# A hybrid attention layer on one core: the first transfers in smaller pieces, and the first row of the first contraction ordered by part

## The chip, the cores and the metric

The kernel runs on one core of a Trainium2 chip. The metric is the device time of one execution in microseconds. Five engines work beside one another, each through its own list of instructions, and wait for one another by semaphores: TensorE (PE, products; PEld is its weight load), VectorE (DVE), ScalarE (ACT), GpSimd (POOL), and SyncE (SP), which only issues transfers. The order inside each list is written out by hand.

## What is computed

One layer of an encoder, on a batch of 512 tokens and one of 256, with the same weights; all values are 32-bit floats.

```
h = x @ w_in                       # 1024 -> 3328 columns, for eight groups of columns
qa, ka, va, ga, qb, kb, vb, gb = split(h)
out_a = dilated_attention(rope(qa), rope(ka), va) * silu(ga)      # 8 heads of 64
out_b = gqa_attention(axial_rope(rms_norm(qb)), axial_rope(rms_norm(kb)), vb) * silu(gb)
f = concat(out_a, out_b) @ w_out
y = layer_norm(alpha * x + f)
```

## The kernel before

**Three products for one.** Every operand of a product is split into a high part, its value rounded to the format that TensorE reads, and a low part, the difference to the value itself. A product of two operands is made of three on TensorE: low by high, high by low, high by high (`three`, line 519). ScalarE makes the high parts by a copy (`weights_high` line 706, `x_high` line 736), VectorE and GpSimd the low parts by a subtraction (`x_low` line 901; `weights_low` line 906 on VectorE, line 1151 on GpSimd).

**Tiles.** x comes transposed, as 8 rows of the contraction (k = 0 to 7), each 128 partitions by 768 tokens, 384 KB, loaded into `mix_t[:, k, :]`; its parts are `t_hi` and `t_lo`. The weights come as 34 units of 128 partitions by 1024 columns, 512 KB. Units are loaded into `raw` (two slots; units 2 and 3 go into `prob`), and their parts lie in `w_hi` and `w_lo`, three slots each.

**The first stage.** `natural(chunk, k)` (line 528) multiplies row k of x, six tiles of 128 tokens, with the weights of a chunk: chunk 0 is the keys and values of mixer B (256 columns, units 0 and 1, four rows k in each), chunks 1 and 2 have 512 columns and two rows to a unit. Each of the six tiles has a PSUM bank, and adds up over k. For each k the order is tile by tile, with the three products of a tile behind one another. Before a row TensorE waits for the low part of that row of x (line 534) and for the low part of the weights (lines 536 and 538). Then follow further projections, run between the steps of the attention, the attention itself, the output product and the layer norm.

**The order at the start.** ScalarE issues the first half of unit 0 on its own queue (line 826; 512 columns, rows k = 0 and 1). SyncE issues, one after another: x of rows 0 and 1, the second half of unit 0, x of rows 2 and 3, unit 1, x of rows 4 to 7, unit 2, tables, unit 3 and the rest. Unit 4 takes the slot of unit 0, and so waits until both low halves of unit 0 are made (line 475). ScalarE then makes the high parts in this order: first half of unit 0, x 0, x 1, second half of unit 0, x 2, x 3, unit 1, x 4 to x 7, units 2 and 3. VectorE makes the low part of the first half of unit 0 and then of x 0 to x 7 (line 1058), GpSimd that of the second half (line 1225) and of units 1 to 3. `hi_count`, `on_dve` and `lo_taken` (lines 282 to 292) work out the counts that each of the semaphores must have reached.

In this document row k (row 0, row 1, ...) is a step of the contraction; [rows 3] is a group of rows of the trace.

Of the kernel before, what the change touches and what calls it, by code (L numbers as in the profile page):

```python
# [7 lines left out]
F32 = mybir.dt.float32  # L8
F32R = mybir.dt.float32r
ALU = mybir.AluOpType  # L10
# [4 lines left out]
P = 128  # L15
# [25 lines left out]
UW = 1024  # L41
# [114 lines left out]
def build(nc, xt, x_prompt, x_sample, weights, q_norm, k_norm, ln_g, ln_b, consts, consts_b, y_prompt, y_sample):  # L156
    ctx = ExitStack()
    with ctx:
# [3 lines left out]
        def sem(name):  # L162
            return ctx.enter_context(nc.semaphore(name))
# [47 lines left out]

        x_loaded = [sem(f"x_loaded{k}") for k in range(KT)]
        ident_loaded, consts_loaded, tables_loaded = sem("ident_loaded"), sem("consts_loaded"), sem("tables_loaded")
        raw_first = sem("raw_first")
        raw_loaded = [sem(f"raw_loaded{i}") for i in range(EARLY)]
        xt_hi, xt_lo = sem("xt_hi"), sem("xt_lo")
        w_hi_done, w_lo_pool, w_lo_dve = sem("w_hi_done"), sem("w_lo_pool"), sem("w_lo_dve")
# [61 lines left out]
            return tuple(a[at // 512][:, at % 512:at % 512 + n] for a in (hi, lo))  # L279


        def hi_count(g, half=1):
            return half + 1 if g == 0 else g + 2

        def on_dve(g, half=0):
            return (g == 0 and half == 0) or NAT_UNITS > g >= KV_UNITS + Q_UNITS or (g >= FIRST_OUT + 3 and g % 2 == 0)

        def lo_taken(g, half=1):
            order = [(0, 0), (0, 1)] + [(n, 1) for n in range(1, UNITS_W)]
            upto = order[:order.index((g, half)) + 1]  # L290
            mine = on_dve(g, half)
            return (w_lo_dve if mine else w_lo_pool), sum(1 for n, s in upto if on_dve(n, s) == mine)


# [172 lines left out]
        def _(sp):  # L467
# [3 lines left out]
            def load_unit(g):  # L471
                if g >= EARLY:
                    sp.wait_ge(*lo_taken(raw_before(g)))
                if g == EARLY:
                    sp.wait_ge(*lo_taken(0, 0))
                sp.dma_start(raw_slot(g), weights[g]).then_inc(raw_arrival(g)[0], 16)

            load_x(0)
            load_x(1)
            sp.dma_start(raw_slot(0)[:, 512:UW], weights[0][:, 512:UW]).then_inc(raw_loaded[0], 16)  # L480
            load_x(2)
            load_x(3)
            load_unit(1)
# [34 lines left out]
        def _(pe):  # L518
# [6 lines left out]
            def x_cols(k, cols):  # L525
                return t_hi[:, k, cols], t_lo[:, k, cols]

            def natural(chunk, k):
                width = 2 * KV_WIDTH if chunk == 0 else CW
                rows = UW // width  # L530
                first, n_units = natural_units(chunk)
                g, row = first + k // rows, k % rows
                if chunk == 0:
                    pe.wait_ge(xt_lo, k + 1)
                if g == 0:
                    pe.wait_ge(*lo_taken(0, row * width // 512))
# [123 lines left out]
                if m == KT - 1:  # L660
                    ins.then_inc(acc_ready, 1)

            for k in range(KT):
                natural(0, k)
            for k in range(KT):
                natural(1, k)
# [36 lines left out]

        @block.scalar
        def _(act):
            def weights_high(g, half=None):
                if half == 0:
                    act.wait_ge(raw_first, 16)
                else:
                    act.wait_ge(*raw_arrival(g))  # L710
# [7 lines left out]
                if half is not None:  # L718
                    nc.scalar.activation(hi[half], raw_slot(g)[:, 512 * half:512 * (half + 1)], ACT.Copy) \
                        .then_inc(w_hi_done, 1)  # L720
                else:
                    nc.scalar.activation(both(hi, g), raw_slot(g), ACT.Copy).then_inc(w_hi_done, 1)  # L722

            def both(hi, g):
                n = g - FIRST_OUT - RING
                if n < 0:
                    return w_hi[:, g % RING, :]
                if n == 0:
                    return k_st[:].rearrange("p s a t -> p (s a t)")[:, 0:UW]
                if n == 1:  # L730
                    return q_st[:].rearrange("p s t -> p (s t)")[:, 0:UW]
                if n in (2, 3):
                    return p_hi[:, n - 2].rearrange("p a c -> p (a c)")
                return v_st[:].rearrange("p s t d -> p (s t d)")[:, 0:UW]

            def x_high(k):
                act.wait_ge(x_loaded[k], 16)
# [85 lines left out]
                if kind(b) == "g":  # L823
                    gate_tanh(b, part)

            act.dma_start(raw_slot(0)[:, 0:512], weights[0][:, 0:512]).then_inc(raw_first, 16)
            weights_high(0, 0)
            x_high(0)
            x_high(1)
            weights_high(0, 1)  # L830
            x_high(2)
            x_high(3)
            weights_high(1)
# [59 lines left out]
        def _(dve):  # L893
# [5 lines left out]
                dve.wait_ge(dve_step, links[0])  # L899

            def x_low(k):
                dve.wait_ge(xt_hi, k + 1)
# [3 lines left out]
            def weights_low(g, half=None):  # L906
                dve.wait_ge(w_hi_done, hi_count(g, 1 if half is None else half))
                hi, lo = unit_places(g)
                for n in range(2) if half is None else (half,):
# [145 lines left out]
                    .then_inc(mix_lo_dve, 1)  # L1055

            nc.vector.memset(zero[:], 0.0)
            weights_low(0, 0)
            for k in range(KT):
                x_low(k)  # L1060
            gain_tables()
            for chunk in range(2):
# [80 lines left out]
        def _(pool):  # L1143
# [4 lines left out]
                ins.then_inc(pool_step, 1)  # L1148
                pool.wait_ge(pool_step, links[0])

            def weights_low(g, half=None):
                pool.wait_ge(w_hi_done, hi_count(g, 1 if half is None else half))
                hi, lo = unit_places(g)
                if half is not None:
                    nc.gpsimd.tensor_tensor(lo[half], raw_slot(g)[:, 512 * half:512 * (half + 1)],
                                            hi[half].bitcast(F32), ALU.subtract).then_inc(w_lo_pool, 1)
                    return
# [64 lines left out]
                nc.gpsimd.tensor_tensor(t_lo[:, e, :], mix_t[:, e, :], t_hi[:, e, :].bitcast(F32), ALU.subtract) \  # L1222
                    .then_inc(mix_lo_pool, 1)

            weights_low(0, 1)
            for g in range(1, 4):
                weights_low(g)
            for t in range(TILES):
# [68 lines left out]
```

## Time and profile before

| | us |
|---|---|
| median of 3 runs | 455.47 (453.39 to 456.83) |
| the profiled execution, its own time | 455.87 |
| its span, first instruction to last | 453.9 |
| TensorE busy with products | 408.9 (90%) |
| VectorE, ScalarE, GpSimd busy | 307.2, 233.8, 227.5 |

All times in the rows are from the profiled execution and count from the beginning of its span. A row of the timeline gives start, length, engine, line of the kernel, operation, and what is written from what; in square brackets how long the engine sat idle before it, and what ended that. A product's printed length contains its way through the array, so that products overlap: their rate is read from their starts.

### The profile page before, as it was taken

The numbers are of one execution on the slowest core, as the hardware profiler recorded it, in microseconds if no ns is written. First come the engines' busy times: TensorE is split into PE (matmuls) and PEld (weight loads), VectorE is DVE, ScalarE is ACT, GpSimd is POOL, SyncE is SP. The second block draws the span as 40 slices with busy tenths as digits, with TensorE's granted clock in tenths as the row PEclk, the third lists the DMA queues.
The fourth block names the chain that finished last, engine by engine and source line by source line (L and its number), as shares of the span: only waits on it lengthen the run. The fifth ranks groups of instructions, "written<-read, shape, count | busy, mean of one in ns | idle before, by whom it ended". The sixth has DMA issues, their size and how long they took to land.

```text
span 453.9 us, 6757 instructions
## 1 busy us (share of the span) xinstructions
PE 408.9 (90%) x2350; PEld 354.2 (78%) x2350; DVE 307.2 (68%) x711; ACT 233.8 (52%) x466; POOL 227.5 (50%) x232
## 2 busy tenths in 40 slices
PE   3999999979988999999999999999898499999970
PEld 3988888768977888888879898888787378888860
DVE  4653237946778886676698998875865634554987
ACT  5441044045656766767677575576574746221331
POOL 1655051474655365455548678845753856221221
PEclk9999999989999999999999999999998979999995
DMA  8821201112011011011011011401110134210113
GB/s 301 340 76 55 75 17 48 47 56 83 4 46 45 3 48 45 3 46 48 2 46 48 1 46 48 140 5 43 48 46 3 46 134 191 92 48 0 71 73 134
DMA packets 10112, 30.11 MB, mean 66 GB/s; under 512 B 1376, under 2 KB 1504, under 8 KB 10080
## 3 DMA queue, kind: packets, MB, share of 16 engines
q1 hardware_dynamic: 9936, 29.43, 18.5%
q8 instruction: 19, 0.31, 0.3%
q10 hardware_dynamic: 144, 0.26, 0.2%
q14 instruction: 13, 0.11, 0.1%
HBM read 26.54 MB, written 3.15 MB: 65 GB/s over the span
## 4 chain that ended last, share of the span: by engine, by line
PE 51%; DVE 26%; issue 8%; ACT 8%; POOL 5%; DMA 1%; DVEq 0%; ACTq 0%; POOLq 0%
PE bank L521 13%; PE bank L522 12%; PE bank L523 12%; PE bank L637 6%; PE bank L568 4%; DVE prob L996 3%; DVE p_lo L1010 3%; ACT prob L782 2%; DVE k_st L976 2%; POOL w_lo L1159 2%; DVE h L1129 2%; DVE q_st L976 2%; ACT w_hi L722 2%; DVE mix_t L1017 2%; PE bank L596 1%
## 5 line engine op out<-in xcount | busy, mean ns | idle before, releaser
L1209 POOL TENSOR_SCALAR prob<-prob,den 128x512 f32<-128x512 f32 (+1 forms) x96 | 68.1, 716 | 60.1 <-DVE den L1005 59.9
L521 PE MATMUL bank<-t_hi,w_lo 128*128 128x512 f32 (+1 forms) x256 | 87.5, 342 | 1.5 <-POOL w_lo L1159 1.5
L523 PE MATMUL bank<-t_hi,w_hi 128*128 128x512 f32 (+1 forms) x256 | 87.0, 340 | 0.0
L522 PE MATMUL bank<-t_lo,w_hi 128*128 128x512 f32 (+1 forms) x256 | 87.0, 340 | 0.0
L1159 POOL TENSOR_TENSOR w_lo<-raw,w_hi 128x512 fp32r<-128x512 f32 x44 | 60.9, 1407 | 49.3 <-ACT w_hi L722 49.3
L791 ACT ACTIVATE p_hi<-bank 128x512 fp32r<-128x512 f32 x80 | 47.8, 597 | 67.9 <-PE bank L568 67.0
L521 PE MATMUL bank<-w_hi,t_lo 128*128 128x512 f32 (+1 forms) x180 | 67.4, 374 | 13.9 <-DVE t_lo L903 7.9
L1010 DVE TENSOR_TENSOR p_lo<-bank,p_hi 128x512 fp32r<-128x512 f32 x80 | 55.1, 689 | 36.3 <-ACT p_hi L791 35.2
L782 ACT ACTIVATE prob<-prob,nmax 128x512 f32<-128x512 f32 (+1 forms) x96 | 62.1, 647 | 32.6 <-DVE nmax L996 32.0
L522 PE MATMUL bank<-w_lo,t_hi 128*128 128x512 f32 (+1 forms) x180 | 66.6, 370 | 0.0
L523 PE MATMUL bank<-w_hi,t_hi 128*128 128x512 f32 (+1 forms) x180 | 66.4, 369 | 0.0
L637 PE MATMUL bank<-p_hi,v_st 128*128 128x256 f32 x160 | 46.5, 308 | 13.1 <-DVE p_lo L1010 8.8
L521 PEld LDWEIGHTS bank<-t_hi,w_lo 128*128 128x128 f32 x256 | 48.7, 190 | 7.9 <-POOL w_lo L1159 1.7
L522 PEld LDWEIGHTS bank<-t_lo,w_hi 128*128 128x128 f32 x256 | 48.8, 191 | 6.2
L523 PEld LDWEIGHTS bank<-t_hi,w_hi 128*128 128x128 f32 x256 | 48.8, 190 | 5.7
L521 PEld LDWEIGHTS bank<-w_hi,t_lo 128*128 128x128 f32 x180 | 35.4, 197 | 19.7 <-DVE t_lo L903 7.9
L568 PE MATMUL bank<-cst,prob 128*128 128x128 f32 x320 | 48.0, 272 | 0.1
L722 ACT ACTIVATE w_hi<-raw 128x1024 fp32r<-128x1024 f32 x26 | 27.3, 1051 | 34.8 <-PE bank L523 19.5
L568 PEld LDWEIGHTS bank<-cst,prob 128*128 128x128 f32 x320 | 38.7, 140 | 7.4 <-POOL prob L1209 0.5
L637 PEld LDWEIGHTS bank<-p_hi,v_st 128*128 128x128 f32 x160 | 30.5, 191 | 16.9 <-issue 11.1
L523 PEld LDWEIGHTS bank<-w_hi,t_hi 128*128 128x128 f32 x180 | 35.4, 197 | 5.4
L522 PEld LDWEIGHTS bank<-w_lo,t_hi 128*128 128x128 f32 x180 | 35.5, 197 | 5.0
(137 smaller groups left out, 771.5 us busy)
## 6 DMA issues: line engine op xcount, KB each, us to landing
raw<-weights SPq DMA_DIRECT2D x31, 512.0 KB, 3.3
mix_t<-xt SPq DMA_DIRECT2D x8, 384.0 KB, 7.1
h<-x_prompt SPq DMA_DIRECT2D x4, 512.0 KB, 5.2
y_prompt<-h SPq DMA_DIRECT2D x8, 256.0 KB, 2.0
prob<-weights SPq DMA_DIRECT2D x2, 512.0 KB, 10.8
h<-x_sample SPq DMA_DIRECT2D x2, 512.0 KB, 8.7
y_sample<-h SPq DMA_DIRECT2D x4, 256.0 KB, 2.0
cst<-consts SPq DMA_DIRECT2D x1, 960.0 KB, 11.2
```

Of the source, the lines that this page charges most:

```text
L521: nc.tensor.matmul(out, a_lo, b_hi, start=first, stop=False)
L522: nc.tensor.matmul(out, a_hi, b_lo, start=False, stop=False)
L523: return nc.tensor.matmul(out, a_hi, b_hi, start=False, stop=last)
L568: ins = nc.tensor.transpose(dst[:, n * P:(n + 1) * P], src, ident)
L637: ins = nc.tensor.matmul(out, lhs, rhs, start=(n == 0 and rhs is hi), stop=(last and rhs is hi))
L722: nc.scalar.activation(both(hi, g), raw_slot(g), ACT.Copy).then_inc(w_hi_done, 1)
L782: ins = nc.scalar.activation(s, s, ACT.Exp, scale=-1.0, bias=nmax[:, j % 2, t:t + 1], accum_out=den[:, j % 2, t:t + 1])
L791: nc.scalar.activation(p_hi[:, slot, at, :], pt_ps[u % 2][:], ACT.Copy).then_inc(pt_hi_done, 1)
L976: nc.vector.tensor_tensor(by_tile(lo), src, by_tile(hi.bitcast(F32)), ALU.subtract).then_inc(staged_lo, 1)
L1010: nc.vector.tensor_tensor(p_lo[:, slot, at, :], pt_ps[u % 2][:], p_hi[:, slot, at, :].bitcast(F32), ALU.subtract).then_inc(pt_lo_done, 1)
L1159: ins = nc.gpsimd.tensor_tensor(lo[n], raw_slot(g)[:, 512 * n:512 * (n + 1)], hi[n].bitcast(F32), ALU.subtract)
L1209: ins = nc.gpsimd.tensor_scalar(s, s, den[:, j % 2, t:t + 1], 0.5, ALU.mult, ALU.mult)
```

## The change

Unit 0 is cut into three pieces (256, 256 and 512 columns) instead of two halves. The first belongs to row 0, the second to row 1, the third to rows 2 and 3. x of row 0 is loaded in two halves of 384 tokens (three tiles each) and rounded in two halves; its low part is still made at once. Row 0 has an order of its own, `first_row`: all six tiles high by high, then six high x by low weights, then six low x by high weights, each group behind its own wait. Rows 1 to 7 are done as before. VectorE makes the low parts of the first two pieces, with x 0 between them, GpSimd that of the third.

```diff
+        STARTS = (slice(0, 256), slice(256, 512), slice(512, UW))
...
-            load_x(0)
+            sp.dma_start(mix_t[:, 0, 0:3 * P], xt[:, 0, 0:3 * P]).then_inc(x_first, 16)
+            sp.dma_start(mix_t[:, 0, 3 * P:TOK], xt[:, 0, 3 * P:TOK]).then_inc(x_loaded[0], 16)
+            sp.dma_start(raw_slot(0)[:, STARTS[1]], weights[0][:, STARTS[1]]).then_inc(raw_second, 16)
             load_x(1)
-            sp.dma_start(raw_slot(0)[:, 512:UW], weights[0][:, 512:UW]).then_inc(raw_loaded[0], 16)
+            sp.dma_start(raw_slot(0)[:, STARTS[2]], weights[0][:, STARTS[2]]).then_inc(raw_loaded[0], 16)
             load_x(2)
...
                 if g == EARLY:
-                    sp.wait_ge(*lo_taken(0, 0))
+                    sp.wait_ge(*lo_taken(0, 1))
...
+            def first_row():
+                w_h, w_l = weight(0, 0, 2 * KV_WIDTH)
+                pe.wait_ge(w_hi_done, hi_count(0, 0))
+                for t in range(TILES):
+                    if t == 0:
+                        pe.wait_ge(x_first_hi, 1)
+                    elif t == 3:
+                        pe.wait_ge(xt_hi, 1)
+                    x_h, x_l = x_cols(0, slice(t * P, (t + 1) * P))
+                    nc.tensor.matmul(bank[t][:, 0:2 * KV_WIDTH], x_h, w_h, start=True, stop=False)
+                pe.wait_ge(*lo_taken(0, 0))
+                for t in range(TILES):
+                    x_h, x_l = x_cols(0, slice(t * P, (t + 1) * P))
+                    nc.tensor.matmul(bank[t][:, 0:2 * KV_WIDTH], x_h, w_l, start=False, stop=False)
+                pe.wait_ge(xt_lo, 1)
+                for t in range(TILES):
+                    x_h, x_l = x_cols(0, slice(t * P, (t + 1) * P))
+                    nc.tensor.matmul(bank[t][:, 0:2 * KV_WIDTH], x_l, w_h, start=False, stop=False)
...
-            for k in range(KT):
+            first_row()
+            for k in range(1, KT):
                 natural(0, k)
...
+            def first_high(step):
+                act.wait_ge((raw_first, raw_second, raw_loaded[0])[step], 16)
+                cols = STARTS[step]
+                nc.scalar.activation(w_hi[:, 0, cols], raw_slot(0)[:, cols], ACT.Copy).then_inc(w_hi_done, 1)
...
+            def first_x_high():
+                act.wait_ge(x_first, 16)
+                nc.scalar.activation(t_hi[:, 0, 0:3 * P], mix_t[:, 0, 0:3 * P], ACT.Copy).then_inc(x_first_hi, 1)
+                act.wait_ge(x_loaded[0], 16)
+                nc.scalar.activation(t_hi[:, 0, 3 * P:TOK], mix_t[:, 0, 3 * P:TOK], ACT.Copy).then_inc(xt_hi, 1)
...
-            act.dma_start(raw_slot(0)[:, 0:512], weights[0][:, 0:512]).then_inc(raw_first, 16)
-            weights_high(0, 0)
-            x_high(0)
+            act.dma_start(raw_slot(0)[:, STARTS[0]], weights[0][:, STARTS[0]]).then_inc(raw_first, 16)
+            first_high(0)
+            first_x_high()
+            first_high(1)
             x_high(1)
-            weights_high(0, 1)
+            first_high(2)
...
-            weights_low(0, 0)
-            for k in range(KT):
+            first_low(0)
+            x_low(0)
+            first_low(1)
+            for k in range(1, KT):
                 x_low(k)
...
-            weights_low(0, 1)
+            first_low(2)
```

How this moves the instructions is shown at two places; a row is a line of the kernel, an operation, what is written from what, its size, and in brackets the semaphores it waits for. On TensorE, at the beginning of its list, row 0 of chunk 0 stands before the change as triples (w_lo, t_hi and so on are the parts):

```order
L521 MATMUL bank<-w_hi,t_lo 128x256 [waits w_lo_dve,xt_lo]
L522 MATMUL bank<-w_lo,t_hi 128x256
L523 MATMUL bank<-w_hi,t_hi 128x256
L521 MATMUL bank<-w_hi,t_lo 128x256
L522 MATMUL bank<-w_lo,t_hi 128x256
```

and with the change, up to the first triple of row 1:

```order
L543 MATMUL bank<-w_hi,t_hi 128x256 [waits x_first_hi,w_hi_done]
L543 MATMUL bank<-w_hi,t_hi 128x256 x2
L543 MATMUL bank<-w_hi,t_hi 128x256 [waits xt_hi]
L543 MATMUL bank<-w_hi,t_hi 128x256 x2
L547 MATMUL bank<-w_lo,t_hi 128x256 [waits w_lo_dve]
L547 MATMUL bank<-w_lo,t_hi 128x256 x5
L551 MATMUL bank<-w_hi,t_lo 128x256 [waits xt_lo]
L551 MATMUL bank<-w_hi,t_lo 128x256 x5
L526 MATMUL bank<-w_hi,t_lo 128x256 [waits w_lo_dve,xt_lo]
```

The 18 products of the row are the same; the one wait that stood ahead of all of them is now four. On ScalarE, whose list begins with the first transfer of weights, this stands before:

```order
L826 DMA raw<-weights 128x512
L719 ACT_TABLE_LOAD
L719 ACTIVATE w_hi<-raw 128x512 [waits raw_first]
L738 ACTIVATE t_hi<-mix_t 128x768 [waits x_loaded0]
L738 ACTIVATE t_hi<-mix_t 128x768 [waits x_loaded1]
L719 ACTIVATE w_hi<-raw 128x512 [waits raw_loaded0]
L738 ACTIVATE t_hi<-mix_t 128x768 [waits x_loaded2]
```

and this with the change:

```order
L856 DMA raw<-weights 128x256
L735 ACT_TABLE_LOAD
L735 ACTIVATE w_hi<-raw 128x256 [waits raw_first]
L762 ACTIVATE t_hi<-mix_t 128x384 [waits x_first]
L764 ACTIVATE t_hi<-mix_t 128x384 [waits x_loaded0]
L735 ACTIVATE w_hi<-raw 128x256 [waits raw_second]
L768 ACTIVATE t_hi<-mix_t 128x768 [waits x_loaded1]
L735 ACTIVATE w_hi<-raw 128x512 [waits raw_loaded0]
L768 ACTIVATE t_hi<-mix_t 128x768 [waits x_loaded2]
```

Two roundings of whole tiles have become four of parts, and from x of row 2 on the list is the old one.

## Rows read from the trace of the kernel before

**Rows 1.** The chain that ended last, by engine, share of the span

```profile
PE 51%; DVE 26%; issue 8%; ACT 8%; POOL 5%; DMA 1%; DVEq 0%; ACTq 0%; POOLq 0%
```

**Rows 2.** The same chain in order of time, its beginning: start, length, what

```profile
0.73 4.74 DMA raw<-weights
...
5.50 0.63 ACT w_hi L719
6.12 0.74 ACT t_hi L738
...
6.89 0.97 DVE t_lo L903
...
7.90 0.58 PE bank L521
```

**Rows 3.** Waits of TensorE, 0 to 100 us: in total, times, longest

```profile
PE bank L521 <- DVE t_lo L903: 7.9, 1, 7.9
PE bank L521 <- POOL w_lo L1159: 1.5, 1, 1.5
```

**Rows 4.** Timeline of TensorE, its second product: start, length, line, operation

```profile
8.28 0.41 PE L522 MATMUL bank<-w_lo,t_hi 128*128 128x256 f32 x1
```

**Rows 5.** Busy time (instructions) by stretch, PE first; last: PEclk, transfer share, GB/s

```profile
0.00:3.50 3.50, 0.00 (x0) 0.00 (x0) 0.06 (x1) 1.28 (x1) 0.20 (x4) 1.00 0.46 78
3.50:4.50 1.00, 0.00 (x0) 0.00 (x0) 0.00 (x0) 0.00 (x0) 0.00 (x0) 1.00 1.04 369
...
7.90:12.55 4.65, 4.65 (x22) 4.65 (x22) 3.48 (x4) 3.84 (x6) 2.61 (x2) 1.00 1.03 413
12.55:20.00 7.45, 7.45 (x63) 7.45 (x63) 6.06 (x5) 3.49 (x4) 5.34 (x4) 1.00 0.80 309
```

**Rows 6.** Transfers by issue, up to 2 us: KB each, median us to landing

```profile
mix_t<-xt SPq DMA_DIRECT2D x1, 384.0 KB, 4.6
...
mix_t<-xt SPq DMA_DIRECT2D x2, 384.0 KB, 5.0
...
raw<-weights SPq DMA_DIRECT2D x1, 256.0 KB, 5.6
```

**Rows 7.** Timeline of SyncE's queue, its first issues

```profile
0.74 0.85 SPq L469 DMA_DIRECT2D mix_t<-xt  x2
1.64 0.42 SPq L480 DMA_DIRECT2D raw<-weights  x1
```

**Rows 8.** ScalarE's groups by shape, up to 100 us: busy, mean ns, idle before

```profile
L738 ACT ACTIVATE t_hi<-mix_t 128x768 fp32r<-128x768 f32 x8 | 6.6, 841 | 0.6
L744 ACT ACTIVATE hkv<-bank 128x256 f32<-128x256 f32 x6 | 2.2, 383 | 4.6 <-PE bank L523 4.6
...
L719 ACT ACTIVATE w_hi<-raw 128x512 fp32r<-128x512 f32 x2 | 1.2, 622 | 3.0 <-DMA raw<-weights 3.0
```

**Rows 9.** Timeline of ScalarE, VectorE and GpSimd, 6 to 15 us

```profile
6.03 1.56 ACT L738 ACTIVATE t_hi<-mix_t 128x768 fp32r<-128x768 f32 x2
...
8.19 1.67 POOL L1155 TENSOR_TENSOR w_lo<-raw,w_hi 128x512 fp32r<-128x512 f32 x1 [7.75 <-ACT w_hi L719]
...
9.10 2.45 DVE L903 TENSOR_TENSOR t_lo<-mix_t,t_hi 128x768 fp32r<-128x768 f32 x2 [0.38 <-ACT t_hi L738]
...
11.61 3.27 POOL L1159 TENSOR_TENSOR w_lo<-raw,w_hi 128x512 fp32r<-128x512 f32 x2 [1.75 <-ACT w_hi L722]
```

**Rows 10.** Timeline of VectorE, its two operations on 256 columns

```profile
18.82 1.30 DVE L918 TENSOR_TENSOR gate<-gate,norms 128x256 f32<-128x256 f32 x1 [1.39 <-DMA norms<-k_norm]
...
20.55 0.43 DVE L918 TENSOR_TENSOR gate<-gate,norms 128x256 f32<-128x256 f32 x1
```

**Rows 11.** Busy time by stretch, where the granted clock (last but two) first fell

```profile
97.80:101.40 3.60, 3.60 (x12) 2.77 (x11) 1.56 (x1) 0.00 (x0) 2.69 (x2) 0.53 0.47 146
```

**Rows 12.** The chain in order of time, 97 to 103 us

```profile
98.47 0.43 PE bank L521
...
102.19 0.24 PE bank L522
```

More of the change, by code:

```diff
@@ L213, in build @@
         ident_loaded, consts_loaded, tables_loaded = sem("ident_loaded"), sem("consts_loaded"), sem("tables_loaded")
-        raw_first = sem("raw_first")
+        raw_first, raw_second, x_first, x_first_hi = (sem("raw_first"), sem("raw_second"), sem("x_first"),
+                                                      sem("x_first_hi"))
         raw_loaded = [sem(f"raw_loaded{i}") for i in range(EARLY)]
@@ L279, in weight, with hi_count, on_dve, lo_taken @@
             return tuple(a[at // 512][:, at % 512:at % 512 + n] for a in (hi, lo))
[L282 to L291, printed above, removed]
+        STARTS = (slice(0, 256), slice(256, 512), slice(512, UW))
+        def hi_count(g, step=2):
+            return step + 1 if g == 0 else g + 3
+        def on_dve(g, step=2):
+            return (g == 0 and step < 2) or NAT_UNITS > g >= KV_UNITS + Q_UNITS or (g >= FIRST_OUT + 3 and g % 2 == 0)
+        def lo_taken(g, step=2):
+            order = [(0, 0), (0, 1), (0, 2)] + [(n, 2) for n in range(1, UNITS_W)]
+            upto = order[:order.index((g, step)) + 1]
+            mine = on_dve(g, step)
             return (w_lo_dve if mine else w_lo_pool), sum(1 for n, s in upto if on_dve(n, s) == mine)
@@ L535, in natural @@
                 if g == 0:
-                    pe.wait_ge(*lo_taken(0, row * width // 512))
+                    pe.wait_ge(*lo_taken(0, min(row, 2)))
                 elif row == 0:
@@ L705, in _, with weights_high @@
         def _(act):
[L706 to L710, printed above, removed]
+            def first_high(step):
+                act.wait_ge((raw_first, raw_second, raw_loaded[0])[step], 16)
+                cols = STARTS[step]
+                nc.scalar.activation(w_hi[:, 0, cols], raw_slot(0)[:, cols], ACT.Copy).then_inc(w_hi_done, 1)
+            def weights_high(g):
+                act.wait_ge(*raw_arrival(g))
                 if RING <= g < FIRST_OUT + RING:
@@ L717, in weights_high @@
                 hi = unit_places(g)[0]
[L718 to L722, printed above, removed]
+                nc.scalar.activation(both(hi, g), raw_slot(g), ACT.Copy).then_inc(w_hi_done, 1)
             def both(hi, g):
@@ L901, in x_low @@
             def x_low(k):
+                if k == 0:
+                    dve.wait_ge(x_first_hi, 1)
                 dve.wait_ge(xt_hi, k + 1)
@@ L904, in x_low, with first_low, weights_low @@
                     .then_inc(xt_lo, 1)
-            def weights_low(g, half=None):
-                dve.wait_ge(w_hi_done, hi_count(g, 1 if half is None else half))
+            def first_low(step):
+                dve.wait_ge(w_hi_done, hi_count(0, step))
+                cols = STARTS[step]
+                nc.vector.tensor_tensor(w_lo[:, 0, cols], raw_slot(0)[:, cols], w_hi[:, 0, cols].bitcast(F32),
+                                        ALU.subtract).then_inc(w_lo_dve, 1)
+            def weights_low(g):
+                dve.wait_ge(w_hi_done, hi_count(g))
                 hi, lo = unit_places(g)
-                for n in range(2) if half is None else (half,):
+                for n in range(2):
                     ins = nc.vector.tensor_tensor(lo[n], raw_slot(g)[:, 512 * n:512 * (n + 1)], hi[n].bitcast(F32),
@@ L1149, in after, with first_low, weights_low @@
                 pool.wait_ge(pool_step, links[0])
-            def weights_low(g, half=None):
-                pool.wait_ge(w_hi_done, hi_count(g, 1 if half is None else half))
+            def first_low(step):
+                pool.wait_ge(w_hi_done, hi_count(0, step))
+                cols = STARTS[step]
+                nc.gpsimd.tensor_tensor(w_lo[:, 0, cols], raw_slot(0)[:, cols], w_hi[:, 0, cols].bitcast(F32),
+                                        ALU.subtract).then_inc(w_lo_pool, 1)
+            def weights_low(g):
+                pool.wait_ge(w_hi_done, hi_count(g))
                 hi, lo = unit_places(g)
[L1154 to L1157, printed above, removed]
                 for n in range(2):
```

## The prediction

> **What bounds the kernel now.** I read the chain of work that ended last first. It is half TensorE and a quarter VectorE, and transfers hold only 1% of it [rows 1]. In order of time it begins with one transfer, the first half of the first weight unit: 4.74 us from its issue at 0.73 [rows 2]. Behind it stand three steps in a row, each on whole tiles: ScalarE rounds 512 weight columns (5.50), then 768 columns of x (6.12), VectorE subtracts to get the low part of x (6.89), and the first product starts at 7.90. From then on the chain is products. The list of TensorE's waits says the same: of all its idle time up to 100 us, 7.9 us stand before the first product, and the next entry has 1.5 us [rows 3]. So whatever starts the first product earlier moves the whole program, if two things hold: the operands of the later rows must not become the new wait, and TensorE must work at the same rate.
>
> The rate has two levels in the timeline. Between 7.90 and 12.55 stand 22 products of 256 columns; behind a first spacing of 0.38 (7.90 to 8.28 [rows 4]) that is 4.27 us for 20 spacings, 0.213 us each, or 256 columns at 1.2 GHz. From 12.55 to 20.00 stand 63 in 7.45 us, 0.12 us each: the level of 2.4 GHz [rows 5]. The lower level lasted 4.65 us, counted from the first product. (The table by stretches prints a granted clock of 1.00 for both; the spacing tells them apart.)
>
> **The first transfers.** Before, 256 KB of weights and 384 KB of x must land: 5.47, and 0.74 + 4.6 = 5.34 us [rows 2, 6]. After, 128 KB and 192 KB are enough for the first product. The table by stretches shows the transfer engines 46% busy up to 3.5 us, moving 3.5 x 78 = 273 KB, and full from then on, at 369 KB a microsecond [rows 5]. So 320 KB had been moved at 3.5 + 47 / 369 = 3.63, and 640 KB at 4.50, 0.87 us later. Pieces of the later transfers were among those bytes, before, and will be after; and shorter rows carry more overhead each. I take 0.72 us: landing at 4.75. No row shows loads of rows this short. The bounds: nothing gained (the slow beginning, not the bytes, sets 5.47; a later landing is excluded, since the same engines move fewer bytes ahead of it), or 1.2 us, when the slow beginning shrinks too. The value lies near the byte count because from 3.5 us on the engines are full.
>
> SyncE issues two transfers more ahead of x of row 1; two take 0.85 us on its queue [rows 7]. So everything behind them is issued that much later. That is hidden by the queue itself: x of row 1, issued about 1.17, took 5.4 us (the median over it and the first, 4.6, is 5.0) [rows 6], and the engines are full from 3.5 us, so work is queued there and issues are not lacking. If that cover were gone, x of row 1 would come at 7.4 instead of 6.6; rounding and subtracting take 1.8 us (0.84 [rows 8] and 0.97 [rows 2]), and TensorE wants it at 9.66, so it still fits.
>
> **From landing to the first product.** Before, 7.90 - 5.47 = 2.43 us. After, the first product needs only two roundings, of 256 and of 384 columns. 256 columns take ScalarE 0.38 us, 512 take 0.62, 768 take 0.84 [rows 8]; so 0.40 for the first (bounds 0.38 and 0.62) and 0.50 for the second, between 0.38 and 0.62. With 0.03 us at the front, an overlap of 0.1 that the two roundings at 5.50 and 6.03 show [rows 9], and 0.04 to the product: 0.03 + 0.40 - 0.10 + 0.50 + 0.04 = 0.87, or 0.9. That saves 1.53 us; together with the transfers 2.25. The first product starts at 5.65.
>
> **Does the first row then run without waits?** The new order is six products high by high, six with the low weights, six with the low x, at 0.213 us (first spacing 0.38): the groups start at 5.65, 7.3 and 8.6, and row 0 ends at 9.66. Product 4 (6.46) wants the second half of x: it lands 192 / 369 = 0.5 us after the first, at about 5.3, and is rounded from 5.6 to 6.1. The low weights: VectorE, 256 columns, 0.43 us [rows 10], from 5.2 to 5.65, against 7.3. The low x: 0.95 us from 6.14, done 7.1, against 8.6. None waits, by 0.3 to 1.6 us. A 256-column subtraction has also taken 1.30 us (beside GpSimd) [rows 10]; then the low x is done at 8.0, still in time. No product is added: 18 before, 18 after.
>
> **And the later rows?** VectorE does the second weight quarter after the low x (7.1 to 7.5) and the low x of row 1 by 8.5. Row 1 is wanted at 9.66. ScalarE is back in its old order by 7.5, since the transfers up to there are the same 1280 KB (the last of them landed at 1.64 + 5.6 = 7.24 [rows 6, 7]). So from row 2 on the operands come as before: GpSimd's half of unit 0 by 9.86, low x of rows 2 and 3 by 11.55, unit 1's low parts by 14.88 [rows 9]. If the lower clock again lasts 4.65 us, to 10.30, TensorE has done 21 products by then and begins row 2 at about 12.1, row 3 at 14.3 and row 4 at 16.4. The least cover is 1.5 us, at row 4. Were it gone, the late microseconds would be lost one for one. SyncE's wait ahead of unit 4 has a further condition (the second weight quarter on VectorE, 7.5), but the GpSimd half ends at 9.8 as before, so unit 5 and the mask table queued behind it move by nothing. What stands behind hangs on TensorE and shifts with it.
>
> The sum: 455.87 (span 453.9 and 2.0 around it) - 2.25 = 453.62 for the profiled execution. The median of the three runs shown is 0.40 lower, 455.47. I count from 455.65, half way: **453.4 us**.
>
> **Rivals.**
> A. The transfers land no sooner, since the beginning of the transfers and not the bytes sets 5.47. For it: up to 3.5 us the engines are not full [rows 5]. Against it: 320 KB are more than the 273 KB that had moved by then. Only 2.43 - 0.9 = 1.53 us stay: 454.1. The Trainium skill ("DMA: Bandwidth & Descriptors", section "Anatomy of one DMA — SWDGE (gpsimd) path") gives a transfer a fixed part of about 2.0 us plus its bytes at 436 GB/s, for transfers issued by GpSimd; by it halving 256 KB saves only an estimated 0.3 us, and the sum would be 1.8 us. The 4.74 us of the row do not agree with the 2.6 us which that gives for 256 KB, because two queues share the engines here.
>
> B. TensorE's clock rises at 12.55 all the same, not 4.65 us after the first product. Then by 12.55 there are 1 + (12.55 - 6.03) / 0.213 = 31.6 products done instead of 21, and 10.6 x 0.12 = 1.3 us are gained: 454.4. If it rises 2 us sooner after the first product than it did, each microsecond is worth 1 - 0.12 / 0.213 = 0.44: gain 3.1, 452.5 (C). One trace can't tell these apart from the forecast. The Trainium skill ("TensorE: Matmul & The Clock Gate", Part 1, "What's actually happening") says that the rise isn't tied to a kernel's start and moves by about half a microsecond from run to run; no run here shows it yet.
>
> D. The slower side: the clock rises much later, because the three groups of row 0 wait for one another (for the second half of x, or the low x) and TensorE idles between them. The place is row 0 and 1; the price is 0.44 us for each microsecond of delay. The new start is used up when the rise comes at 15.45, where 1 + (T - 6.03) / 0.213 products equal 21 + (T - 12.55) / 0.12. At 20 us the time is 457.7; if the lower clock held for all 144 products of the first chunk, that chunk would end at 36.5 instead of 27.3, and the time would be about 465. Against it: the working above finds no wait in row 0. For it: the least reserve is 0.3 us, at product 4.
>
> Apart from these, the granted clock fell in the middle of the program, first to 0.53 between 97.8 and 101.4, where TensorE had waited just before [rows 3, 11]; there products took 0.43 instead of 0.24 us [rows 12], 8 of them, 1.5 us. One such stretch more or less is about what the three runs (453.39 to 456.83) differ by, and moves any of the cases.
>
> **How the numbers follow.** Forecast 0.57, A 0.17, B 0.12, C 0.06, D 0.08. The range: from C less one stretch of low clock (452.5 - 1.5) to B with most of one more (454.4 + 1.2): 451.0 to 455.6. About 1% (4.6 us) is what a measurement can tell from no change. Faster by more than that needs C and a vanished low stretch together (451.0): 0.04. Slower by more needs D far beyond its point: 0.03. Within 1%: 0.93.
>
> **What would show it.** Right: the first transfer's landing at 4.4 to 5.0; the first product at 5.4 to 6.0, high by high; no TensorE wait in rows 0 to 7 but the first; the evacuations of the first chunk beginning about 2.2 us sooner; the rest shifted by as much. Wrong: a landing still near 5.4 (A); 0.213 us spacing up to 12.5 (B) or beyond 15 (D); a TensorE wait for the low parts of unit 1 at row 4; or a shift at 25 us that is gone again at the end.

## The result, and the profile after

The changed kernel takes 453.78 us (median of 15 runs, 450.5 to 455.38), the kernel before, beside it on the same chip, 456.83 (15 runs, 453.39 to 458.17). The ratio is 0.9931, with a 95% interval of 0.9906 to 0.9956. Timed a second time on another occasion the ratio was 0.9950 (0.9927 to 0.9973). Forecast were 453.4 us and, as a ratio, 0.9951 (2.25 of 455.65).

| | before | after |
|---|---|---|
| profiled execution, us | 455.87 | 454.04 |
| its span | 453.9 | 452.3 |
| first weights landed (issue at 0.73) | 5.47 | 4.2 |
| first product | 7.90 | 5.19 |
| unit 1 rounded from | 10.48 | 11.68 |
| first evacuation of chunk 0 | 25.78 | 23.32 |

An evacuation is ScalarE's copy of a finished tile out of its PSUM bank. The first ones of chunk 0, before and after:

```profile
25.78 2.18 ACT L744 ACTIVATE hkv<-bank 128x256 f32<-128x256 f32 x6 [4.57 <-PE bank L523]
```

```profile
23.32 2.18 ACT L774 ACTIVATE hkv<-bank 128x256 f32<-128x256 f32 x6 [1.00 <-PE bank L528]
```

The beginning came out sooner than forecast. The transfers by issue of the changed kernel (KB each, us to landing), as in [rows 6]:

```profile
mix_t<-xt SPq DMA_DIRECT2D x1, 192.0 KB, 3.3
raw<-weights ACTq DMA_DIRECT2D x1, 128.0 KB, 3.5
```

and the timeline behind them on ScalarE and TensorE, where before there were [rows 2]:

```profile
4.22 0.42 ACT L735 ACTIVATE w_hi<-raw 128x256 fp32r<-128x256 f32 x1 [1.77 <-DMA raw<-weights]
4.54 0.51 ACT L762 ACTIVATE t_hi<-mix_t 128x384 fp32r<-128x384 f32 x1
...
5.19 1.62 PE L543 MATMUL bank<-w_hi,t_hi 128*128 128x256 f32 x6 [5.19 <-ACT t_hi L762]
...
6.61 1.48 PE L547 MATMUL bank<-w_lo,t_hi 128*128 128x256 f32 x6
...
7.89 1.02 PE L551 MATMUL bank<-w_hi,t_lo 128*128 128x256 f32 x6
```

The three groups of row 0 follow one another without a wait. The second takes 1.48 us (five spacings of 0.213 and the length of the last product); the third takes only 1.02, since the clock rises within it: the spacing first shortens behind the product at 8.10 (7.89 + 0.213), 2.9 us after the first product, where it had been 4.65 before.

Then TensorE does wait, first a little, at row 1. Its low x is finished at 8.74, no later than before (6.89 + 1.83 = 8.72), but the row is wanted sooner:

```profile
7.78 0.96 DVE L936 TENSOR_TENSOR t_lo<-mix_t,t_hi 128x768 fp32r<-128x768 f32 x1 [0.92 <-ACT t_hi L768]
...
8.80 0.39 PE L526 MATMUL bank<-w_hi,t_lo 128*128 128x256 f32 x1
```

The product before it began at 8.63 and the next one begins at 9.02, where two spacings of 0.12 would have given 8.87: some 0.15 us are lost, which the list of waits doesn't show, because the printed length of the earlier product covers them. The list of its waits up to 100 us, against [rows 3]:

```profile
PE bank L543 <- ACT t_hi L762: 5.2, 1, 5.2
PE bank L526 <- POOL w_lo L1202: 2.2, 2, 1.5
```

GpSimd's entry has grown from one wait of 1.5 us to two. The timeline of GpSimd and TensorE around row 4 shows the new one:

```profile
12.81 3.25 POOL L1202 TENSOR_TENSOR w_lo<-raw,w_hi 128x512 fp32r<-128x512 f32 x2 [2.83 <-ACT w_hi L746]
...
15.25 0.28 PE L528 MATMUL bank<-w_hi,t_hi 128*128 128x256 f32 x1
...
16.21 0.36 PE L526 MATMUL bank<-w_hi,t_lo 128*128 128x256 f32 x1 [0.68 <-POOL w_lo L1202]
```

It stands before row 4: the next product would have followed at 15.37, and came at 16.21, 0.84 us later, behind low parts that were finished at 16.06 (14.88 in [rows 9]). Unit 1 is late. The chain that ended last now has another beginning than in [rows 2]:

```profile
4.01 7.65 DMA raw<-weights
...
11.68 1.07 ACT w_hi L746
```

It no longer runs over the first product, but over SyncE's issues, which stand ahead of these lines, and the transfer of unit 1. And ahead of that transfer the engines had stood partly idle. Stretches of half a microsecond (the last two columns are transfer share and GB/s):

```profile
5.00:5.50 0.50, 0.31 (x1) 0.34 (x2) 0.09 (x1) 0.50 (x3) 0.00 (x0) 1.00 0.87 250
5.50:6.00 0.50, 0.50 (x4) 0.50 (x4) 0.43 (x1) 0.27 (x1) 0.00 (x0) 1.00 0.42 123
6.00:6.50 0.50, 0.50 (x4) 0.50 (x4) 0.50 (x2) 0.00 (x0) 0.00 (x0) 1.00 0.55 162
```

The share falls to 0.42, with x of row 1 and three more transfers issued long before (2.11 to 3.5 us). I call this the hole.

In sum, at the first evacuation: 2.71 us from the earlier start, 0.8 from the earlier clock ((4.65 - 2.91) x 0.44), less 0.84 at row 4 and 0.15 at row 1, makes 2.5; measured are 25.78 - 23.32 = 2.46. At 95 us the shift is still the same: the wait that was at 97.36 before stands at 94.91. Behind that it is moved by stretches of low clock, which fell at other places (below), and by 0.5 us near 217 us, where TensorE waited 0.7 us for VectorE in the attention, against 0.2 before; at the end the profiled executions are 1.83 us apart.

### The profile page after: what moved, and what is told of

Same layout as the page of the kernel before. It is cut to its first block, busy times and chain, and to the rows that moved or that the text cites. A ratio compares the mean times of both kernels' runs of the same rounds, so it can differ in the third digit from the quotient of the medians.

```text
span 452.3 us, 6763 instructions
## 1 busy us (share of the span) xinstructions
PE 408.9 (90%) x2350; PEld 353.7 (78%) x2350; DVE 307.1 (68%) x712; ACT 234.3 (52%) x468; POOL 226.3 (50%) x232
## 4 chain that ended last, share of the span: by engine, by line
PE 49%; DVE 26%; issue 9%; ACT 7%; POOL 6%; DMA 2%; SPq 1%; DVEq 0%; ACTq 0%; POOLq 0%
PE bank L526 12%; PE bank L528 12%; PE bank L527 12%; PE bank L662 5%; PE bank L593 4%; POOL w_lo L1202 3%; DVE prob L1035 3%; DVE p_lo L1049 3%; ACT prob L812 2%; DVE k_st L1015 2%; ACT w_hi L746 2%; DVE h L1170 2%; DVE q_st L1015 2%; DMA raw<-weights 2%; DVE mix_t L1056 2%
## 5 line engine op out<-in xcount | busy, mean ns | idle before, releaser
L526 PE MATMUL bank<-w_hi,t_lo 128*128 128x512 f32 (+1 forms) x174 | 64.7, 372 | 6.7 <-POOL t_lo L1265 5.7
L527 PE MATMUL bank<-w_lo,t_hi 128*128 128x512 f32 (+1 forms) x174 | 64.0, 368 | 0.0
L528 PE MATMUL bank<-w_hi,t_hi 128*128 128x512 f32 (+1 forms) x174 | 64.0, 368 | 0.0
L526 PEld LDWEIGHTS bank<-w_hi,t_lo 128*128 128x128 f32 x174 | 33.2, 191 | 12.7 <-issue 7.0
L528 PEld LDWEIGHTS bank<-w_hi,t_hi 128*128 128x128 f32 x174 | 33.3, 191 | 5.4
L527 PEld LDWEIGHTS bank<-w_lo,t_hi 128*128 128x128 f32 x174 | 33.3, 191 | 5.0
## 6 DMA issues: line engine op xcount, KB each, us to landing
prob<-weights SPq DMA_DIRECT2D x2, 512.0 KB, 10.9
```

Source lines behind the costliest of these rows:

```text
L526: nc.tensor.matmul(out, a_lo, b_hi, start=first, stop=False)
L527: nc.tensor.matmul(out, a_hi, b_lo, start=False, stop=False)
L528: return nc.tensor.matmul(out, a_hi, b_hi, start=False, stop=last)
```

## The experiments

All but the first and the last, which are the changed kernel itself, are edits of one of the two kernels, or of a kernel edited before. Ratios are to the kernel before, run beside each.

**The changed kernel again**, without an edit.

> The changed kernel once more, one look. My theory: the hole in the transfers between 5 and 6.5 us (engines 40 to 55% busy), the landing of unit 1 at about 11.6 instead of 10.45, and TensorE's wait of 0.7 us for unit 1's low parts at row 4 belong to the kernel, since x of row 1 and all behind it is issued 0.9 us later. All three come again, and the first product starts at 5.0 to 5.4. Rival: the hole was an accident of one execution; then unit 1 lands by 10.9 and row 4 does not wait. On the clock: if its rise is tied to the first product it comes again 3.0 us after it; if it is not, the distance differs from 2.98 by half a microsecond or more.

Measured: 450.36 us. First product at 5.06, the hole again (0.61, 0.48, 0.80 in the half microseconds from 5.0), unit 1 rounded from 11.24. The clock rose in row 1: the spacing first shortens behind the product at 10.53, 5.5 us after the first product, and row 4 did not wait. So the hole belongs to the kernel; the wait at row 4 came only where the clock rose early; and the clock's rise isn't tied to the first product. By the sum above, 2.84 us from the start less 0.4 for the later clock make 2.5; the first evacuation came at 23.27, 2.51 us sooner.

**The order alone.** The kernel before, with the row of the new order and waits for the whole tiles:

```diff
-            for k in range(KT):
+            first_row()        # waits: xt_hi 1, lo_taken(0, 0), xt_lo 1
+            for k in range(1, KT):
                 natural(0, k)
```

> The kernel before with the new order of row 0 alone (high by high, then low weights, then low x; transfers and roundings whole as before). My theory: the first product follows the rounding of x at 6.9 to 7.0 instead of 7.9, unit 1 lands at 10.4 to 10.6 as before, row 4 doesn't wait; gain 0.9 to 1.0 us, ratio about 0.998. Rival, that only an earlier landing counts and the low x sets row 0 in any order: ratio 1.000, with a TensorE wait for the low x inside row 0.

Measured: first product at 7.04, no wait in row 0, ratio 0.9976 (0.9955 to 0.9998). As expected, but for unit 1, rounded from 10.76 with the same transfers as before.

**The pieces alone.** The changed kernel, with row 0 by triples:

```diff
-            first_row()
-            for k in range(1, KT):
+            for k in range(KT):
                 natural(0, k)
```

> The changed kernel with its pieces, but row 0 in the old order by triples behind the low x. My theory: landing at 4.0 to 4.2 as in the changed kernel, first product behind the low x of row 0 at 6.5 to 6.6, unit 1 again near 11.6, so the wait at row 4 shrinks to nothing or 0.2 us unless the clock rises early; gain 1.3 us from the start, ratio about 0.997. Rival, that the order does nearly all of it: ratio 1.000 and the first product later than 7.4.

Measured: landing at 4.4, first product at 6.75, unit 1 rounded from 11.35, no wait at row 4, ratio 0.9971 (0.9948 to 0.9994). As expected, but for the landing and the first product, 0.2 later. Together the two parts give more at the start (2.71 us) than one by one (0.86 + 1.15): only with both can the first product run on a half of x without its low part.

**The second pieces from ScalarE.** The changed kernel:

```diff
-            sp.dma_start(mix_t[:, 0, 3 * P:TOK], ...).then_inc(x_loaded[0], 16)
-            sp.dma_start(raw_slot(0)[:, STARTS[1]], ...).then_inc(raw_second, 16)
...
+            act.dma_start(mix_t[:, 0, 3 * P:TOK], ...).then_inc(x_loaded[0], 16)
+            act.dma_start(raw_slot(0)[:, STARTS[1]], ...).then_inc(raw_second, 16)
             first_high(0)
```

> The changed kernel, with the second piece of weights and the second half of x issued by ScalarE behind its first transfer, so that SyncE issues x of row 1 and all behind it at the times of before. My theory (late issue makes the hole): x of row 1 lands by 6.7 and unit 1 by 10.8 us, the engines stay above 80% between 5 and 6.5 us, row 4 does not wait, and the first product still starts at 5.2 to 5.7; gain 0.5 to 0.9 us over the changed kernel, ratio 0.989 to 0.992. Rival (short rows and the number of transfers make the hole, whoever issues them): unit 1 lands at 11.3 or later, row 4 waits as in the changed kernel, and the ratio is 0.993 or worse.

Measured: the hole is gone. In the profile of this kernel:

```profile
5.50:6.00 0.50, 0.50 (x3) 0.50 (x3) 0.00 (x0) 0.08 (x1) 0.00 (x0) 1.00 1.05 395
6.00:6.50 0.50, 0.36 (x2) 0.07 (x2) 0.00 (x0) 0.45 (x1) 0.00 (x0) 1.00 1.09 416
```

Unit 1, issued at 3.3, landed 6.8 us later and is rounded from 10.53, against 11.68 and 11.24 in the changed kernel, with the same number of small transfers. So the rival falls: small pieces as such do not make the hole. But the second half of x and the second weights now landed late. The first group of row 0 took 2.13 us, where it took 1.62 in the changed kernel:

```profile
5.38 2.13 PE L541 MATMUL bank<-w_hi,t_hi 128*128 128x256 f32 x6 [5.38 <-ACT t_hi L760]
```

The second weights were rounded from 7.48 instead of 5.37, which held up the low x of row 1, and another 0.3 us were lost there (products at 9.36, 9.68 and 9.90, with 0.12 as the spacing). That is as much as the earlier unit 1 could give back at row 4. The ratio is 0.9955 (0.9931 to 0.9979); the gain of 0.5 to 0.9 us that I expected did not show.

**The low parts of unit 1 signalled by halves.** The changed kernel; only GpSimd's signals and two waits of TensorE change:

```diff
                 for n in range(2):
                     ins = nc.gpsimd.tensor_tensor(lo[n], ...)
+                    if g == 1 and n == 0:
+                        ins.then_inc(w_lo_pool, 1)
                 ins.then_inc(w_lo_pool, 1)
```

> The changed kernel; GpSimd signals the low parts of unit 1 after each of its two halves, and TensorE waits at row 4 for the first half and at row 6 for the second. My theory: unit 1 still lands at 11.2 to 11.7 us, the first half of its low parts is ready at about 14.0 to 14.5, so row 4 doesn't wait even if the clock rises 3 us after the first product; the gain over the changed kernel is 0.8 us where it does rise so early and nothing where it rises late, some 0.3 us on average: ratio 0.990 to 0.994. Rival: the wait goes to row 6 or to the low x of row 4, and TensorE stands 0.5 us or more between 14 and 20 us.

Measured: ratio 0.9925 (0.9906 to 0.9944), no wait in rows 0 to 7. But in this profile the clock rose late (first shorter spacing behind the product at 10.34, 5.1 us after the first product), and GpSimd's second half, done at 16.13 (12.87 + 3.26), would hardly have held up row 4, which began at 16.2. Neither theory is decided by it, and the ratio can't be told from the changed kernel's.

**The same, and one piece of weights from ScalarE** (the halves of x stay with SyncE).

```diff
-            sp.dma_start(raw_slot(0)[:, STARTS[1]], ...).then_inc(raw_second, 16)
+            act.dma_start(raw_slot(0)[:, STARTS[1]], ...).then_inc(raw_second, 16)
```

> As the last, and the second piece of weights is issued by ScalarE behind the first; the halves of x stay with SyncE. My theory (one queue with many small transfers leaves the engines short of work): SyncE has one transfer fewer ahead of x of row 1, which lands by 6.6; unit 1 lands at 10.6 to 11.2, the hole between 5 and 6.5 us is smaller (no half microsecond under 0.6), the first product starts at 5.1 to 5.4 and no product of rows 0 to 7 waits: ratio 0.989 to 0.993. Rival (any split costs the same wherever it is issued): unit 1 at 11.2 or later as in the changed kernel.

Measured: first product at 5.39; x of row 1 at 6.35 and unit 1 at 10.35 are rounded; no half microsecond from 4.5 to 6.5 under 0.90. The theory's side, and better than it said for unit 1. Ratio 0.9950 (0.9933 to 0.9967), short of the expected range: an earlier unit 1 is worth nothing while row 4 doesn't wait for it.

**x of row 0 in one transfer** (rounded in halves all the same).

```diff
-            sp.dma_start(mix_t[:, 0, 0:3 * P], ...).then_inc(x_first, 16)
-            sp.dma_start(mix_t[:, 0, 3 * P:TOK], ...).then_inc(x_loaded[0], 16)
+            load_x(0)
```

> The changed kernel with x of row 0 in one transfer again (rounded in halves as in the changed kernel). The halves of x: x of row 0 lands at 4.5 to 4.9 instead of 4.0, so the first product starts at 5.5 to 5.9 instead of 5.1 to 5.2. Theory 2 (small pieces on one queue): one transfer fewer, so the hole shrinks and unit 1 lands at 10.6 to 11.1. Theory 1 (late issue): x of row 1 is issued 0.47 us earlier than in the changed kernel, which gives 11.0 to 11.3. Rival: the split of x brings nothing, and the first product starts at 5.3 or sooner.

Measured: the weights are rounded from 4.92 instead of 4.22, the first product starts at 5.89, and unit 1 is rounded from 10.88, with stretches of 0.54 and 0.66. So the split of x is worth 0.7 us at the start, and costs 0.4 to 0.8 us at unit 1 (11.24 and 11.68 in the two profiles of the changed kernel above). x of row 1 was issued at 1.65 here.

**Two small transfers ahead of x of row 1**, in the kernel before.

```diff
             load_x(0)
+            sp.dma_start(norms[:, 0, :], q_norm[None, :].to_broadcast([P, HEAD_DIM])).then_inc(tables_loaded, 16)
+            sp.dma_start(norms[:, 1, :], k_norm[None, :].to_broadcast([P, HEAD_DIM])).then_inc(tables_loaded, 16)
             load_x(1)
```

> The kernel before, with the two small transfers of the norm gains (32 KB each) issued by SyncE between x of row 0 and x of row 1: later issue alone, without pieces. Theory 1, the later issue by 0.9 us makes the hole: unit 1 lands at 11.2 or later and some half microsecond between 5 and 6.5 us has the engines under 0.8 busy. Theory 2, the pieces are so small that the engines finish them sooner than one queue hands over the next: x of row 0, still whole, keeps the engines at work, there is no hole, and unit 1 lands at 10.5 to 10.9, later only by the bytes. The first product starts at 7.8 to 8.0 either way.

Measured: the greatest hole of all, and x of row 1 was rounded at 8.51 instead of about 6.8:

```profile
4.50:5.00 0.50, 0.00 (x0) 0.00 (x0) 0.00 (x0) 0.00 (x0) 0.00 (x0) 1.00 0.08 22
5.00:5.50 0.50, 0.00 (x0) 0.00 (x0) 0.00 (x0) 0.48 (x1) 0.00 (x0) 1.00 0.06 16
```

Two microseconds are more than an issue that is 0.94 us later explains, and theory 2, in which whole x covers the gap, is wrong. I took it that a queue hands over every transfer at a pace of its own, and asked that of the next. (The first product came at 7.42: the first weights landed 4.3 us after their issue, at 5.0 instead of 5.47.)

**The same two, issued by ScalarE:**

```diff
+            act.dma_start(norms[:, 0, :], ...).then_inc(tables_loaded, 16)
+            act.dma_start(norms[:, 1, :], ...).then_inc(tables_loaded, 16)
             weights_high(0, 0)
```

> The kernel before, with the two small transfers of the norm gains issued by ScalarE behind its first transfer of weights, so that the same small transfers go ahead of x of row 1, but on the other queue. My theory (one queue hands its transfers over at a pace of about 1 us each, whatever their size, and small ones leave the engines without work): SyncE's queue has its transfers of before, x of row 1 lands at 6.4 to 6.9 and unit 1 at 10.3 to 10.9 us, and no half microsecond between 4 and 6.5 us has the engines under 0.8. Rival (rows of 256 bytes hold up the engines themselves, on any queue): the hole comes again, x of row 1 lands at 7.5 or later and unit 1 at 11.5 or later.

Measured: a hole again, later. The second half of unit 0, issued by SyncE at 1.65, is rounded only from 9.12, and unit 1 from 12.86; x of row 1 was in time, so that the rival holds for unit 1 alone. So these two transfers, whose 128 rows of 256 bytes come from one place, hold up the others on either queue. The theory fell as put, and the experiment before it says nothing on later issue.

**Later issue alone**, in the kernel before: SyncE waits for an operation of VectorE on a tile that is free.

```diff
             load_x(0)
+            sp.wait_ge(held, 1)
             load_x(1)
```

> The kernel before, in which SyncE waits for an operation of VectorE on a spare tile before it issues x of row 1, at about 2.05 instead of 1.17 us. Ahead of it stand the same 640 KB as in the changed kernel, in two transfers instead of four, so that late issue stands alone, with no further transfer and no small rows. Theory L (late issue leaves the engines without work): unit 1 lands at 11.0 to 11.7 us as in the changed kernel, with some half microsecond between 4.5 and 6.5 us under 0.8 busy. Theory Q (one queue does not hand over several small transfers fast enough): unit 1 lands at 10.3 to 10.8 us and the engines stay above 0.85. The first product starts at 7.8 to 8.1 either way.

Measured: x of row 1 was issued at 1.89 (0.72 us later, not 0.88), unit 1 is rounded from 11.00, and no half microsecond from 4 to 6.5 us is under 0.87 busy. In between: 0.2 to 0.5 us lost at unit 1 (10.48 before; 10.76 in the run of the order alone, with the same transfers), as by theory L, and no hole, as by theory Q. So late issue may cost a part of the 0.8 to 1.2 us that unit 1 lost, but it doesn't make the hole: with x of row 0 whole the hole came although x of row 1 was issued sooner, at 1.65. It goes with how the bytes are divided between the queues. Every kernel with the hole had only 128 KB on ScalarE's queue at the start, every kernel without it 256 KB or more (the two runs with the norm gains apart). The nearest pair is the run with x of row 0 whole and the run with one piece of weights from ScalarE: x of row 1 is issued at 1.65 and at 1.64, behind the same 640 KB, and only the first has the hole, though the second has two small pieces ahead of it on SyncE's queue. Why this leaves the engines idle stays open.

**Half signals for unit 10 too.** In every trace TensorE waits 1.5 us at about 95 us for the low parts of the first unit of the next stage (unit 10), which GpSimd makes in two halves; four of the eight rows need only the first. On the kernel with half signals and two queues:

```diff
-                    if g == 1 and n == 0:
+                    if g in (1, NAT_UNITS) and n == 0:
...
+                if (b, part, k) == (0, 0, KT // 2):
+                    pe.wait_ge(*lo_taken(g))
```

> The kernel with half signals and two queues, and the same half signal for unit 10, the first unit of the next stage, whose low parts TensorE waits 1.5 us for at about 95 us in every trace so far. My theory: the first half is ready 1.2 us sooner, the wait at 95 us falls from 1.5 to 0.2 or 0.3 us, and the time by 1.2 us, or more where the granted clock no longer falls there: ratio 0.986 to 0.992. Rival: the wait moves to the fifth row of that block, which needs the second half, and nothing is gained: ratio as without it, 0.992 to 0.995.

Measured: 451.62 us, ratio 0.9882 (0.9842 to 0.9922). The wait has shrunk as expected; before, and here:

```profile
97.36 0.50 PE L521 MATMUL bank<-t_hi,w_lo 128*128 128x512 f32 x1 [1.51 <-POOL w_lo L1159]
```

```profile
93.20 0.50 PE L525 MATMUL bank<-t_hi,w_lo 128*128 128x512 f32 x1 [0.29 <-POOL w_lo L1208]
```

It has the lowest median of all that were timed over several runs. Its interval stands clear of the kernel before and of the kernel that it edits (0.9933 to 0.9967); with the changed kernel's two intervals (0.9906 to 0.9956, 0.9927 to 0.9973) it still meets the first. Between the two medians lie some 3 us; the wait explains 1.2 of them, and what gives the rest isn't shown.

**The changed kernel, timed once more.**

> The changed kernel once more, timed. My theory: the gain stands in the first 25 us alone, 2.3 to 2.6 us at the first evacuation (25.78 before), and the rest of the differences are stretches of low clock: ratio 0.991 to 0.996. The hole between 5 and 6.5 us comes a third time, and row 4 waits only if the clock rises within 4 us of the first product. Rival: the gain of 3 us in the median is the kernel's own beyond the start; then the shift grows between 25 us and the end in this execution too, at places without a change of the granted clock.

Measured: ratio 0.9950, the hole a third time (0.59), first product at 5.21, first evacuation at 23.47 (2.31 us sooner), no wait at row 4 with the clock rising 5.7 us after the first product (behind the product at 10.90); at the end the span is 2.1 us shorter than the first profile of before. Product by product the shift stays at 2.3 us up to 95 us, and behind that it changes by more than 0.1 us only in stretches of low clock of one execution or the other. As expected, so that the gain is the start's.

## Why the prediction was right

The time and the ratio lie in the range. The working behind them was right in its mechanism at the start, too small in its size there, and wrong behind it, at the transfers and the clock. That the errors nearly cancel is luck: in the first profile the larger start and the early clock are taken back at row 4 and row 1 (2.46 us in place of 2.25), in the other two the larger start by a later clock (2.51 and 2.31). Of the signs named beforehand, the landing (4.2 instead of 4.4 to 5.0) and the first product (5.06 to 5.21 instead of 5.4 to 6.0) came too soon, a wait for the low parts of unit 1 at row 4, named as a sign of being wrong, came in one profile of three, and the shift at the first evacuation came as written.

**The chain up to the first product** was right as a mechanism and too small by a fifth: 2.71 us instead of 2.25. From the beginning of the first rounding to the first product it took 5.19 - 4.22 = 0.97 us where 0.87 had been worked out; the 0.1 stands between ScalarE's last rounding (4.54 + 0.51 = 5.05) and the product, 0.14 us where 0.04 had been taken from a step of VectorE. The transfers were mis-sized: 0.72 us was taken, within 0 to 1.2, and 1.27 measured. The upper bound was even passed. Rival A is out, and the slow beginning does shrink with the pieces: up to 3.5 us the engines moved 105 KB a microsecond, against 78 before [rows 5], at the same busy share of 0.46. What the other queue carries counts too, as rival A had it: the same 128 KB of weights took 3.5 us beside the halves of x, and 4.2 beside x of row 0 whole.

**No wait in row 0** was right: all three profiles of the changed kernel show the three groups back to back. The groups had been placed at 7.3 and 8.6, which the spacings named there do not give: with 0.38 and then 0.213 from 5.65 on they begin at 7.1 and 8.4, and the end of the row at 9.66 is right. The reserves were 0.2 us smaller than written, and still there.

**"Work is queued there and issues are not lacking"** is the step that failed. With whole tiles queued the engines were full from 3.5 us in [rows 5]; with pieces in their place they ran dry at 5.5 us, and unit 1 came 0.8 to 1.2 us later. I had noted that x of row 1 would still fit in if this cover went, and had not carried it on to unit 1, whose cover I had put at 1.5 us. With an early clock that was not enough (row 4 was wanted at 15.37, not 16.4, and its low parts came at 16.06, not 14.88), and 0.84 us were lost one for one, as written there. The Trainium skill ("DMA: Bandwidth & Descriptors", section "Issuing engines are not separate DMA queues") says that issuing from several engines only saves the time of issuing. Here one piece moved from SyncE to ScalarE took unit 1 from 11.2 to 11.7 (five profiles) to 10.35, more than the 0.47 us of one issue; the measurement decides.

**The clock's rise** was the open point of B and C. It is not tied to the first product: counted from it as the forecast's 4.65 was, to the first product with a shorter spacing behind it, there were 2.9, 5.5 and 5.7 us in the changed kernel. So C happened in one profile, where what it should have given was taken back at row 4, and in the two others the rise came 0.8 and 1.0 us later than forecast, which at 0.44 us for each microsecond cost some 0.4 us. The Trainium skill ("TensorE: Matmul & The Clock Gate", Part 1, "What's actually happening") has the rise move by about half a microsecond to either side; here it moved by more than two. Nor did it keep its place in the program (B): it came at 8.1, 10.5 and 10.9 us, not at 12.55. D did not come: no wait inside row 0 held the clock back.

**The sum over runs.** The earlier start is 2.3 to 2.5 us at the first evacuation in all three profiles. The medians differed by 3.05 and the second timing by 0.50%, or 2.3 us. These agree within their intervals; that the first is more than the start's gain is left to the spread below.

## What to carry to other kernels

Cut the first transfers so that the first product needs little, and start with the products whose operands need the fewest steps: here each alone gave about 1 us, both together 2.7. Then go on to where the next full tile is wanted: with most of the small pieces on one queue the engines ran dry here, and with one more of them on the other queue they did not, though no time was gained by that alone. And signal a tile by the part that its first reader needs: halving one signal on the critical path brought more in the trace (1.2 us) than anything else tried behind the start.

## What had not been expected

Two executions of one kernel can differ by as much as the change brings, by where the granted clock falls. Two profiles of the changed kernel, alike to 0.05 us at the first evacuation (23.32 and 23.27), ended 3.7 us apart (spans 452.3 and 448.6). The first, by stretches (PE first, granted clock last but two):

```profile
322.20:325.60 3.40, 3.40 (x10) 2.66 (x9) 1.43 (x5) 0.98 (x3) 3.32 (x4) 0.50 0.00 0
```

and the second:

```profile
322.20:325.60 3.40, 3.40 (x21) 2.88 (x20) 1.41 (x5) 1.29 (x4) 3.32 (x4) 1.00 0.00 0
```

Where the first has half the clock, with 10 products begun, the second has 21. The kernel before has such stretches at 98 [rows 11] and twice later, the first of these profiles at 322, 343 and 360, the second at 355 alone. The shift between two executions moves by some 1.6 us where one of them has the stretch at 98 or at 322 and the other hasn't, which is more than half of the whole change; only medians over many runs show the change through it. In these traces what TensorE did before doesn't tell where it comes: both profiles were busy for 2.19 of the 4 us ahead of 322, and the wait of 1.5 us that stood ahead of the stretch at 98 stands at 95 in both of them, without one behind it. And two transfers of 32 KB, of 128 rows of 256 bytes read from one place, held back 256 to 512 KB on either queue by some 2 us.
